# Final norm's weight row spread after the second expert group, its 4 KB lent to an expert weight; an earlier, smaller first refill; constant products in the last expert of a group

## The reference, cut to what matters

```python
# hier_moe: 32 experts in 4 groups; every token goes to 2 experts
hid = jax.nn.silu(xb @ w1[e]) * (xb @ w3[e])      # w1, w3: 1024 x 512
return hid @ w2[e]                                # w2: 512 x 1024
...
x = x + hier_moe(rms_norm(x, g_ffn), ...)
return rms_norm(x, g_final)                       # g_final: 1024 values
```

## Time and profile before

| | us |
|---|---|
| median of 3 runs | 1057.65 |
| lowest, highest | 1056.35, 1058.83 |
| the profiled execution, its own time | 1058.77 |
| its span (first to last instruction) | 1056.7 |
| TensorE busy (share of span) | 918.5 (87%) |
| DMA queue of the loads, share of 16 engines | 75.8% |

### The profile page before, as it was taken

One profiled execution on the slowest core, in us unless ns is written; L12 is line 12 of the kernel. 1 busy time (PEld: TensorE's weight loads), 2 busy tenths in 40 slices (PEclk: granted clock), 3 DMA queues, 4 the chain that ended last, 5 costly groups with the idle time before them and its releaser, 6 DMA issues.

```text
span 1056.7 us, 22572 instructions
## 1 busy us (share of the span) xinstructions
PE 918.5 (87%) x9950; PEld 761.6 (72%) x9950; DVE 498.0 (47%) x807; ACT 385.2 (36%) x553; POOL 21.6 (2%) x24
## 2 busy tenths in 40 slices
PE   9999999999999999999999997787757667575764
PEld 8998887888888888988777885665635546463643
DVE  5646768677676767889887650111100101010101
ACT  5445766464444446756666340000000000000001
POOL 0000002110000000000000000000000000000000
PEclk9999999999999999999999999999898978888987
DMA  9864445545655575665447999999999999999994
GB/s 328 293 194 159 165 136 175 163 150 190 213 162 195 199 254 162 198 202 163 160 170 286 389 401 426 425 425 421 427 427 427 430 429 427 429 427 428 431 428 200
DMA packets 89455, 309.49 MB, mean 293 GB/s; under 512 B 7940, under 2 KB 48696, under 8 KB 76600
## 3 DMA queue, kind: packets, MB, share of 16 engines
q1 hardware_dynamic: 88768, 308.40, 75.8%
q10 hardware_dynamic: 632, 0.29, 0.1%
HBM read 307.63 MB, written 1.05 MB: 292 GB/s over the span
## 4 chain that ended last, share of the span: by engine, by line
PE 62%; DMA 28%; DVE 4%; issue 3%; ACT 1%; POOL 0%; SPq 0%; DVEq 0%; ACTq 0%
DMA arena<-in_w 27%; PE ps L927 12%; PE ps L929 11%; PE ps L928 11%; PE ps L1037 7%; PE ps L1454 7%; PE ps L1041 4%; PE ps L1480 2%; DMA arena<-in_w_in 1%; PE ps L1219 1%; PE ps L1371 1%; DVE w_split L1867 1%; PE ps L1433 1%; PE ps L1417 1%; PE ps L1207 0%
## 5 line engine op out<-in xcount | busy, mean ns | idle before, releaser
L1867 DVE TENSOR_TENSOR w_split<-arena,w_split 128x2048 fp32r<-128x2048 f32 (+1 forms) x69 | 157.2, 2288 | 29.9 <-ACT w_split L1526 29.4
L1454 PE MATMUL ps<-arena,xg 128*32 128x128 f32 x2688 | 104.8, 318 | 74.0 <-DMA arena<-in_w 66.7
L2474 DVE TENSOR_TENSOR hid<-silu_e,ps 128x128 f32<-128x128 f32 x32 | 12.1, 378 | 311.7 <-ACT silu_e L1814 311.7
L1526 ACT ACTIVATE w_split<-arena 128x2048 fp32r<-128x2048 f32 x70 | 132.8, 1901 | 63.7 <-PE ps L929 53.1
L1454 PEld LDWEIGHTS ps<-arena,xg 128*32 128x32 f32 x2688 | 89.3, 129 | 91.8 <-DMA arena<-in_w 79.4
L927 PE MATMUL ps<-w_split,x_both 128*128 128x512 f32 x256 | 102.1, 399 | 0.6 <-DVE expo_pair L2117 0.6
L929 PE MATMUL ps<-w_split,x_both 128*128 128x512 f32 x256 | 99.8, 390 | 0.0
L928 PE MATMUL ps<-w_split,x_both 128*128 128x512 f32 x256 | 99.8, 390 | 0.0
L1814 ACT ACTIVATE silu_e<-ps 128x128 f32<-128x128 f32 x32 | 8.9, 277 | 240.1 <-PE ps L1454 240.1
L1037 PE MATMUL ps<-x_both,w_split 128*128 128x512 f32 x352 | 83.9, 390 | 0.1
L1480 PE MATMUL ps<-arena,hid_T 128*32 128x256 f32 x896 | 61.5, 415 | 24.1 <-DMA arena<-in_w 21.8
(11 more groups left out here) (325 smaller groups left out, 1462.0 us busy)
## 6 DMA issues: line engine op xcount, KB each, us to landing
arena<-in_w SPq DMA_DIRECT2D x65, 2048.0 KB, 26.3
arena<-in_w_in SPq DMA_DIRECT2D x41, 1024.0 KB, 5.2
even_w<-in_w SPq DMA_DIRECT2D x12, 2048.0 KB, 27.0
arena<-in_w_ffn_in SPq DMA_DIRECT2D x22, 1024.0 KB, 5.1
third_w<-in_w SPq DMA_DIRECT2D x6, 2048.0 KB, 16.9
arena<-in_w_ffn_out SPq DMA_DIRECT2D x11, 1024.0 KB, 4.9
arena<-in_w_out SPq DMA_DIRECT2D x8, 1024.0 KB, 6.2
extra_w<-in_w SPq DMA_DIRECT2D x4, 2048.0 KB, 19.0
```

Source lines behind the costliest of these rows:

```text
L1454: last = mm(ps[SLOTS * g:SLOTS * g + SLOTS, 6, P * n:P * n + P], xg[:, c, SLOTS * e:SLOTS * e + SLOTS], places[n][:, c, P * g:P * g + P], ...
L1526: fn(w_hi[:, u % 3, 0:n], ring[:, u % 3, 0:n], ACT.Copy).then_inc(hi_ready, 1)
L1867: v.tensor_tensor(w_lo[:, u % 3, 0:n], ring[:, u % 3, 0:n], w_hi[:, u % 3, 0:n].bitcast(F32), ALU.subtract).then_inc(lo_ready, 1)
L2474: v.tensor_tensor(hid[:, :].rearrange("p (b i) -> p i b", b=4), silu_e[:, :].rearrange("p (i b) -> p i b", b=4), ps[:, 6, P:2 * P].rearran ...
```

## The change

1. `final_row` moves to the place of `next_w1` / `next_w2`, which is free when expert 7's w2 has been used. The 4 KB that it had become `spare_w`, two chunks of an expert weight.
2. The eight spreading products, the two copies on ScalarE and the waits for them move from ahead of the ranks to behind quad 1 (ahead of the loop). ScalarE's quad 1 is written out for this.
3. CHOICE_WARM goes from 7 to 23.
4. Chunks 0 and 1 of expert 4's w3 (512 KB) are loaded to `spare_w`, issued right behind expert 2's w2 and ahead of expert 3's w3. Chunks 2 and 3 (512 KB) follow when two of expert 0's eight w1 chunks are read (`e_w1_part`), chunks 4 to 7 (1 MB) when all eight are, as before.
5. LAST_WARM = 10: in the looped quads, the fourth expert has ten constant products ahead of w1's wait and ten ahead of w3's.

```diff
-CHOICE_WARM = 7
+CHOICE_WARM = 23
+LAST_WARM = 10
...
-    final_row = moe("final_row", [P, D])
+    spare_w = moe("spare_w", [P, 2, EFF])
+    final_row = nc.alloc_sbuf_tensor_at("final_row", [P, D], F32, offset=next_at)
...
         expert_load(2, third_w, 2, in_third3[2])
+        sp.dma_start(spare_w[:, :, :], sources[1][:, 4, 0:2, :]).then_inc(spare_in, 16)
...
         expert_load(3, fourth_w, 1, in_fourth[1])
-        for half, landing in ((0, first_half[1]), (1, landed_w[0][0])):
-            sp.wait_ge((e_w1_half, e_w1)[half], 1)
-            chunk_load(4, next_w, 1, slice(KC // 2 * half, KC // 2 * half + KC // 2), landing)
+        sp.wait_ge(e_w1_part, 1)
+        sp.dma_start(even_w[0][:, 0:2, :], sources[1][:, 4, 2:4, :]).then_inc(first_half[1], 16)
+        sp.wait_ge(e_w1, 1)
+        chunk_load(4, next_w, 1, slice(KC // 2, KC), landed_w[0][0])
...
         keep_warm(CHOICE_WARM, 5)
-        for half in range(2):
-            for j in range(4):
-                c = 44 + 4 * half + j
-                last = mm(ps[:, 4 + half, P * j:P * j + P], vec[:, c:c + 1].to_broadcast([P, P]), ident, start=True,
-                          stop=True)
-            last.then_inc(final_spread, 1)
         pe.wait_ge(route_sel, 1)
-        pe.wait_ge(final_taken, 1)
...
-                pe.wait_ge(final_taken, 2)
                 first_collect(5, (2, 3), xg_half)
...
                 for n in range(2):
+                    if looped and e == QUAD - 1:
+                        keep_warm(LAST_WARM, 5)
...
+                    if not looped and (q, e, n) == (1, 0, 1):
+                        pe.wait_ge(spare_in, 16)
...
+                        source = places[n][:, c, :]
+                        if not looped and (q, e, n) == (1, 0, 1) and c < KC // 2:
+                            source = (spare_w if c < 2 else even_w[0])[:, c % 2, :]
...
+                        if not looped and (q, e, n, c) == (0, 0, 0, 1):
+                            last.then_inc(e_w1_part, 1)
...
-                                last.then_inc(e_w1_half, 1)
...
         quad_body(1)
+        for half in range(2):
+            for j in range(4):
+                c = 44 + 4 * half + j
+                last = mm(ps[:, 4 + half, P * j:P * j + P], vec[:, c:c + 1].to_broadcast([P, P]), ident, start=True,
+                          stop=True)
+            last.then_inc(final_spread, 1)
+        pe.wait_ge(final_taken, 2)
         with pe.Fori(2, n_pass * (EXPERTS // QUAD)) as q:
...
-        for half in range(2):
-            act.wait_ge(final_spread, half + 1)
-            fn(final_row[:, 512 * half:512 * half + 512], ps[:, 4 + half, :], ACT.Copy).then_inc(final_taken, 1)
...
-        with act.Fori(1, n_pass * (EXPERTS // QUAD)) as q:
+        quad_body(1)
+        for half in range(2):
+            act.wait_ge(final_spread, half + 1)
+            fn(final_row[:, 512 * half:512 * half + 512], ps[:, 4 + half, :], ACT.Copy).then_inc(final_taken, 1)
+        with act.Fori(2, n_pass * (EXPERTS // QUAD)) as q:
```

More of the change, by code:

```diff
@@ L555, in layers_kernel @@
     in_third3 = [sem(f"third_w{n}_in") for n in (1, 3, 2)]
-    next_in = sem("next_w1_in")
+    next_in, spare_in = sem("next_w1_in"), sem("spare_w3_in")
     route_in, route_exp = sem("route_in"), sem("route_exp")
@@ L560, in layers_kernel @@
                                                                         "gt_done", "gt_ready"))
-    e_w1, e_w1_half = sem("e_w1"), sem("e_w1_half")
+    e_w1, e_w1_part = sem("e_w1"), sem("e_w1_part")
     final_spread, final_taken = sem("final_gain_spread"), sem("final_gain_taken")
@@ L1452, in quad_body @@
                             pe.wait_ge((xg_part, xg_ready)[c // 4], q + 2)
+                        source = places[n][:, c, :]
+                        if not looped and (q, e, n) == (1, 0, 1) and c < KC // 2:
+                            source = (spare_w if c < 2 else even_w[0])[:, c % 2, :]
                         for g in range(4):
                             last = mm(ps[SLOTS * g:SLOTS * g + SLOTS, 6, P * n:P * n + P],
-                                      xg[:, c, SLOTS * e:SLOTS * e + SLOTS], places[n][:, c, P * g:P * g + P],
+                                      xg[:, c, SLOTS * e:SLOTS * e + SLOTS], source[:, P * g:P * g + P],
                                       start=c == 0, stop=c == KC - 1, tile_position=(0, SLOTS * g))
+                        if not looped and (q, e, n, c) == (0, 0, 0, 1):
+                            last.then_inc(e_w1_part, 1)
                         if not looped and (e, n, c) == (0, 0, KC // 2 - 1):
                             if q == 0:
-                                last.then_inc(e_w1_half, 1)
                                 first_collect(7, (4, 5), xg_done)
@@ L1803, in quad_body @@
         def quad_body(q):
-            e0 = act.snap(q * QUAD) if not isinstance(q, int) else 0
+            e0 = act.snap(q * QUAD) if not isinstance(q, int) else q * QUAD
             act.wait_ge(xg_half, q + 2)
-            if isinstance(q, int):
+            if isinstance(q, int) and q == 0:
                 fn(xg[:, 2:4, :].rearrange("p a b -> p (a b)"), ps[:, 5, 0:2 * P], ACT.Copy).then_inc(xg_part, 1)
```

## The result

The changed kernel takes 1066.39 us (median of 6 runs, 1065.7 to 1067.5) against 1057.47 for the kernel before (6 runs): ratio 1.009, 95% interval 1.0079 to 1.01. It is **slower by 0.9%**, 8.9 us, outside the range of the prediction. The profiled execution took 1067.5 us, its span is 1065.5.

The account below looks back on a forecast made before the run. One stream of weight loads was taken to bound the second half. Late refills +0.35 us and the clock at the end -0.9 sum to -0.55 against the median 1057.65: 1057.1 us, range 1055.2 to 1060.8.

Parts of the forecast that it names:

- part 4: Constant products in each looped quad's last expert: zero in quads 2 to 6, full clock in quad 7, -0.9 us.
- part 3: Spreading behind quad 1: quad 2 begins 4.5 us later, expert 10's w1 lands at 726.0 for 725.65, +0.35 us.
- the slower rival: Quad 2's late first refill finds all 16 engines dry and costs in full: +3.2 us, 1060.8 us, chance 0.2.
- a lag between engines: End of the load stream: the last of 16 DMA engines is 5 us behind the average, 1045.4 against 1040.4.
- Part 1: Constant products ahead of the choice: 46 instructions, 5.4 us, move the choice's next step 1.9 us later.
- Part 2: First refills: quarter issued at 625.4, half at 629.0, landing at 634.1 for 636.0; bounds -1.4 to +2 us.
- The fit that part 2 quotes from the Trainium skill: First refills: about 2.0 us fixed per load, so the extra smaller load costs up to 2 us without overlap.
- the rival with products at half clock: Last quad: constant products at 1.2 GHz run past w3's landing, w2 0.7 us later: +1.05, 1058.7 us, chance 0.1.

Follow-up runs that it names:

- experiment 1: Changed kernel without the last expert's constant products (LAST_WARM 0): 1058.53 us against 1057.09 for the kernel before, ratio 1.001.
- experiment 2: Kernel before with only the last expert's constant products added (10 calls twice): 1057.14 us against 1057.09, ratio 0.9995.
- experiment 5: Changed kernel with CHOICE_WARM back at 7, the last expert's ten products twice kept: 1056.49 us against 1057.19 for the kernel before, ratio 0.9995.
- experiment 6: Kernel before with CHOICE_WARM 23 and the last expert's constant products, nothing else of the change: 1068.0 us, ratio 1.0102.
- experiment 8: Kernel before with the last expert's constant products and CHOICE_WARM 15: 1057.53 us, ratio 1.0001.
- experiment 3: Changed kernel with 40 empty instructions in each of the two places instead of the products; none appear in the trace: 1058.63 us, ratio 1.0016.
- experiment 9: Changed kernel with CHOICE_WARM 7 and the spreading put into banks 6 and 7: 1055.59 us against 1057.19 for the kernel before, ratio 0.999.
- experiment 10: Changed kernel with CHOICE_WARM 7, spreading in banks 6 and 7, and LAST_WARM 0: 1056.95 us against 1057.48 for the kernel before, ratio 0.9994.
- experiment 4: Changed kernel with 2 products of 512 columns per place instead of 10 of 128: 1058.12 us, ratio 1.0007.
- experiment 11: Changed kernel with CHOICE_WARM 7, spreading in banks 6 and 7, and 2 products of 512 columns per place: 1056.14 us against 1057.48, ratio 0.9989.
- experiment 7: Changed kernel with the 20 constant products per pass cut to 8 columns each: 1068.55 us, ratio 1.0112.

## Why the prediction was wrong

**The step that failed** is in part 4, "In quads 2 to 6 loads are issued up to 27 us ahead, so TensorE has room: zero", and its companion in part 3, "32 more instructions of products, 64 with their weight loads, ahead of the loop: zero beside part 1". Both cost instructions by the time that they run and never by the room that they take. No rival had that mechanism either; the slower rival ended at 1060.8 for another reason. What the runs showed in its place is a step in the number and place of the loop's instructions (experiments 1, 2, 5, 6, 8). By their medians, the kernels with 88 packets take 1066 to 1069 us and those with 42 take 1055 to 1059.

The sign of it could have been read before. In the kernel before, 19 packets of q8 come from 620 to 760 us, the unrolled quads and the loop's first pass, and TensorE stops there again and again without a wait that the profile shows. These are from the chain of waits between 630 and 660:

```profile
634.36 1.69 issue
...
641.74 0.68 issue
646.33 2.57 issue
...
654.61 2.30 issue
```

From 760 to 1020, the repeated passes, there is neither a row of q8 nor such a stop, and the same holds for experiment 1. In the changed kernel the rows of that stretch are these:

```profile
q1 hardware_dynamic: 7537, 109.78, 99.6%
q8 instruction: 40, 0.66, 1.0%
```

Over five repeated passes 46 more packets came, 9.2 each, and 0.66 MB in 40 packets is 16 KB each. In the trace a pass is 1693 instructions of TensorE with the constant products and 1613 without them. The Trainium skill, "Runtime: NRT & Kernel Launch", section "Instruction fetch mechanics", gives TensorE 128 KiB of instruction memory, refilled in blocks of 16 KiB, 256 instructions. The packet size seen agrees. As an estimate from these figures, 1693 instructions are 6.6 blocks, so a pass lies in seven or eight of them, and nine packets per pass are more than it covers. One block fetched ahead, beyond the loop's end, would account for that and make the step one of eight against nine blocks; this is my inference and no run measured it. The same section of the Trainium skill calls the memory a FIFO and says that a taken branch to a target outside the current two-page window forces a fetch. Here the measurement decides: the short or early loop branched back over more than six blocks and ran its repeated passes with no fetch.

**How the fetches cost 9 us** is shown in part. From 760 to 1020 the changed kernel moves 109.78 MB of weights, experiment 1 moves 111.41, and the DMA engines are full in both (99.6% and 1.0% for instructions, against 100.7%). The missing 1.63 MB are 3.8 us at 428 GB/s; the instructions' packets account for 1.0% of 260 us, 2.6 us of it. (The rates 425 and 428 show less, since the 425 counts the instructions' bytes too.) That the engines stay full also says that TensorE's 5 us per pass don't reach the average engine: loads are issued some 25 us ahead.

The tail gives the whole. After 1038 the changed kernel still moves 367 x 7 + 204 x 5 + 127 x 5 = 4224 KB, 9.9 us at 428 GB/s, so the average engine is done at 1047.9 and the last load lands at 1055.1: 7.2 us later, where before it was 5.0. In experiment 1 the average engine ends at 1042.6 and the last load (issued 1019.3, 26.9 us) lands at 1046.2: 3.6 later. So 5.3 us of the 8.9 between that run and the changed kernel fall on the average engine and 3.6 on the gap behind it. Of the 5.3, 3.8 are the ones above, and another 0.8 fell in 720 to 726 (369 GB/s for 423).

Two limits. The prediction calls the whole gap a lag between engines; but in the kernel before hardly anything moves from 1043.8 to 1045.4 (18 GB/s), so about 1.6 us of its 5.0 lie between the end of the transfer and the landing. And the gap differs by itself: experiment 3, with as many instructions in its trace as experiment 1, has 1.8 us (1043.3 to 1045.1). So the share of the gap is 3.6 to 5.4 us, and why it grows with the fetches stays open: that the packets of q8 fall unevenly on the 16 engines would fit, but no view shows a packet's engine.

**Part 1** was right: 1.8 us on TensorE for 1.9, and the clock there was full before and after.

**Part 2 and part 3** were right in mechanism and near in size. The sum for both was +0.35 us; experiments 1 and 3 (which hold both and not part 4) give +0.1% and +0.16%, 1.1 to 1.7 us. The mis-sized term is expert 10's w1. In experiment 1 it is issued at 717.06 and lands 9.5 us later, at 726.6, which is +0.9 us for the +0.35 of the sum; in the changed kernel it takes 9.7 us, to 727.7. I had 7.55 us, for an idle queue, and the queue was not idle: the DMA share from 715 to 720 is 0.86 and 0.80. The point on which the sum turned, that the last engine loses less than the average one, holds: in experiment 1 the average engine ends 2.2 us later (1042.6 for 1040.4) and the last landing only 0.8 (1046.2 for 1045.4). The fit that part 2 quotes from the Trainium skill stands on that page in the section "Anatomy of one DMA — SWDGE (gpsimd) path", for DMAs issued by GpSimd. These are issued by SyncE, and nothing in the sum rests on it.

**Part 4's gain** was right as a mechanism and within its bounds. In the changed kernel w3's last products run in 1.96 us and w2 starts at 1054.02, 0.2 us after its landing, where before it was 0.95. As a time, experiment 2 gives 0.9995 (0.9986 to 1.0005) and the pair of experiments 9 and 10 some 0.4 us (0.999 and 0.9994): no more than can be told from nothing, for 0.9 forecast. The changed kernel also showed a part of the rival with products at half clock: 20 of them took 3.25 us ahead of w1, whose products started 1.2 us after its landing (1045.3); w2 still started on time.

```profile
1043.29 3.25 PE L1121 MATMUL ps<-ones 128*128 128x128 f32 x20
1046.47 1.95 PE L1456 MATMUL ps<-arena,xg 128*32 128x128 f32 x64
1048.35 2.50 PE L1121 MATMUL ps<-ones 128*128 128x128 f32 x20
1050.78 1.96 PE L1456 MATMUL ps<-arena,xg 128*32 128x128 f32 x64
...
1054.02 1.93 PE L1483 MATMUL ps<-arena,hid_T 128*32 128x256 f32 x32 [0.21 <-DMA arena<-in_w]
```

## What to carry to other kernels

Price every instruction put into a long loop, and also every one ahead of it, by room as well as by time: look at the instruction queue in the stretch in which the loop repeats. Here it was quiet, so the loop was kept, and a step lay somewhere above its size. When filler work is wanted, make it of few wide instructions (experiments 4 and 11), and look at the trace before calling narrow ones cheap (experiment 7). And where one queue of loads sets the end, read the tail of the rate: the average engine's end and the last landing are two different times, and a hole costs them differently.

## What the runs showed of the hardware

- A loop of TensorE with 80 instructions more per pass and a start 32 instructions later ran with 42 instruction packets (experiment 8); with a start 64 later it took 88, and 10 us more (experiment 6).
- Each repeated pass that fetches begins with 4.2 to 5.8 us in which TensorE stands still (changed kernel, experiments 6 and 7), waiting for nothing that the profile shows. In the unrolled quads, where packets of q8 arrive too, it stopped for 0.7 to 2.6 us at a time (kernel before, 630 to 660).
- A constant f32 product of 8 columns took TensorE as long as one of 128: 20 in 2.40 to 2.73 us against 2.50 (experiments 7 and 9). Four of 512 columns took 1.98 us (experiment 4).
- Holes in the stream of loads cost the average DMA engine more than the last landing. With both holes deeper, the average engine ended 2.2 and 2.9 us later than in the kernel before, and the last landing moved by +0.8 and -0.3 us (experiments 1 and 3, one execution each).
